# Gated linear attention on one Trainium2 core: unread products in TensorE's waits, and the head of the output stage beside the last chunk

## The reference

```python
def step(S, inp):                                  # one chunk of GLA
    b = jnp.cumsum(ax, axis=1)
    diff = b[:, :, None] - b[:, None, :]
    decay = jnp.where(causal, jnp.exp(jnp.minimum(diff, 0.0)), 0.0)
    scores = jnp.einsum('bthc,bshc,btshc->btsh', qx, kx, decay)
    o = jnp.einsum('btsh,bshe->bthe', scores, vx) + jnp.einsum('bthc,bhce->bthe', qx * jnp.exp(b), S)
    b_last = b[:, -1]
    S_new = jnp.exp(b_last)[..., None] * S + jnp.einsum('bshc,bshe->bhce', kx * jnp.exp(b_last[:, None] - b), vx)
...
of, Sf = gla_scan(gq, gk, gv, log_a[:, :, 0], S0[:, 0])
ob, Sb = gla_scan(flip(gq), flip(gk), flip(gv), flip(log_a[:, :, 1]), S0[:, 1])
og = rms_norm((of + flip(ob)), o_gain).reshape(B, T, GLA_WIDTH) * jax.nn.silu(gg)
out = jnp.concatenate([lru, og], axis=-1)
...
x = x + gate * rms_norm(out @ w_out, g)            # the output stage
```

## Time and profile before

| what | value |
| --- | --- |
| median of three runs | 3104.09 us (3102.58 to 3104.70) |
| the profiled execution's own time | 3103.27 us |
| its span, first to last instruction | 3101.5 us |
| mean granted clock of PE | 0.962 of 2.4 GHz |
| busy: PE, DVE, POOL, ACT | 2917.8, 2031.2, 1426.6, 1238.6 us |
| chain that ended last, by engine | PE 66%, POOL 12%, DVE 9% |
| GLA passes 0 to 8 | 2017.5 to 2210.6 us of the span |
| output stage of layer 1, first product | 2226.70 us |

### The profile page before, as it was taken

How to read it: one execution, slowest core, us unless ns; L and a number is a source line. 1 busy time by engine, 2 the same in 40 slices (tenths; PEclk the granted TensorE clock), 3 DMA queues, 4 the chain that set the end, 5 groups by cost and what they waited for, 6 DMA issues and landing times.

```text
span 3101.5 us, 41472 instructions
## 1 busy us (share of the span) xinstructions
PE 2917.8 (94%) x16141; PEld 2504.6 (81%) x16141; DVE 2031.2 (65%) x2488; ACT 1238.6 (40%) x2055; POOL 1426.6 (46%) x1002
## 2 busy tenths in 40 slices
PE   7999988999899999999999999989799999999998
PEld 3898876666689999978877887768689999978877
DVE  3679776554568444587877376578778544488886
ACT  2311164676543222233324477544353332333322
POOL 1121064666434444487851121176433443488870
PEclk9999998999999999999999999966799999999999
DMA  5566574000222323333243323241232323332241
GB/s 207 175 211 221 194 213 148 24 1 28 85 82 79 115 88 113 107 115 116 98 137 98 109 93 135 78 133 54 67 107 74 104 95 108 125 123 74 100 176 61
DMA packets 230880, 346.81 MB, mean 112 GB/s; under 512 B 32118, under 2 KB 124318, under 8 KB 230686
## 3 DMA queue, kind: packets, MB, share of 16 engines
q1 hardware_dynamic: 230686, 344.17, 33.2%
HBM read 259.18 MB, written 84.94 MB: 111 GB/s over the span
## 4 chain that ended last, share of the span: by engine, by line
PE 66%; POOL 12%; DVE 9%; issue 5%; ACT 4%; DMA 2%; SPq 1%; PEldq 0%; POOLq 0%; ACTq 0%; DVEq 0%; PEld 0%
PE psum L1002 19%; PE psum L1194 9%; POOL d_slot L1134 6%; PE psum L662 6%; PE psum L2950 5%; PE psum L1299 3%; PE psum L1647 3%; PE psum L665 3%; PE psum L1176 2%; PE psum L3964 2%; PE psum L439 2%; PE psum L2609 1%; DVE ada_acc L296 1%; PE psum L829 1%; PE psum L2590 1%
## 5 line engine op out<-in xcount | busy, mean ns | idle before, releaser
L1194 PE MATMUL psum<-d_slot 128*128 128x512 f32 x2016 | 468.1, 392 | 8.6 <-DVE yacc L1239 3.7
L1194 PEld LDWEIGHTS psum<-d_slot 128*128 128x128 f32 x2016 | 379.7, 189 | 92.9 <-DVE yacc L1239 5.3
L1002 PE MATMUL psum<-AT,w_slot 128*128 128x288 f32 x2688 | 369.1, 296 | 4.7 <-POOL w_slot L967 4.7
L1002 PEld LDWEIGHTS psum<-AT,w_slot 128*128 128x128 f32 x2688 | 362.6, 189 | 5.1 <-POOL w_slot L967 5.1
L1134 POOL TENSOR_TENSOR d_slot<-down_a,d_slot 128x512 fp32r<-128x512 f32 x168 | 300.1, 1810 | 72.2 <-ACT d_slot L1125 72.0
L591 POOL TENSOR_TENSOR WT<-RAW,WT 128x1024 fp32r<-128x1024 f32 (+3 forms) x30 | 111.1, 3726 | 429.5 <-ACT WT L580 429.5
L662 PE MATMUL psum<-WT,AT 128*128 128x512 f32 (+1 forms) x1296 | 282.5, 378 | 4.0 <-ACT stage L717 4.0
L1002 PE MATMUL psum<-s_hi,w_slot 128*128 128x288 f32 x1344 | 269.0, 295 | 3.3 <-issue 1.7
L662 PEld LDWEIGHTS psum<-WT,AT 128*128 128x128 f32 x1296 | 231.7, 190 | 46.8 <-ACT stage L717 4.3
L967 POOL TENSOR_TENSOR w_slot<-RAW,w_slot 128x512 fp32r<-128x512 f32 x112 | 155.8, 1402 | 224.1 <-ACT w_slot L963 224.1
L1002 PEld LDWEIGHTS psum<-s_hi,w_slot 128*128 128x128 f32 x1344 | 215.3, 188 | 4.1 <-issue 2.1
(11 more groups left out here) (467 smaller groups left out, 6083.6 us busy)
## 6 DMA issues: line engine op xcount, KB each, us to landing
RAW<-ffn_w SPq DMA_DIRECT2D x40, 1024.0 KB, 6.6
ada_raw<-ada_w SPq DMA_DIRECT2D x36, 1024.0 KB, 6.2
hidden<-hid SPq DMA_DIRECT2D x56, 576.0 KB, 3.1
down_a<-hidden SPq DMA_DIRECT2D x48, 512.0 KB, 5.9
RAW<-ffn_w SPq DMA_DIRECT2D x48, 512.0 KB, 7.4
RAW<-w_in_even SPq DMA_DIRECT2D x5, 2048.0 KB, 8.2
RAW<-w_in_odd SPq DMA_DIRECT2D x5, 2048.0 KB, 7.9
mix_x<-x_all SPq DMA_DIRECT2D x18, 512.0 KB, 3.3
```

The costliest lines, as they stand in the source:

```text
L1002: mm = nc.tensor.matmul(psum[:, bank + b, 0:HB], w_slot[p][:, w, k, :], TOKENS[p][x][:, k, b * HB:(b + 1) * HB], start=(begins and k == 0 ...
L1194: mm = nc.tensor.matmul(psum[:, D_RING[q % 3] + pair % 2, :], slot[:, 0, x, k, pair * P:(pair + 1) * P], slot[:, 1, w, k, :], start=(k == ...
```

## The change

Five things are altered, all in layer 1.

- PE issues products that nothing reads: `unread(n)` multiplies 128 x 128 of a weight group with its first 512 columns into bank 6. There are 8 behind `gl_go`, ahead of level 0 of pass 0, 6 behind that, and in every pass 4, 2, 1 and 1 behind levels 2, 3, 4 and 5. Bank 6 is also that of a state update, so PE waits for the backward state behind level 2.
- Tiles 0 and 1 are early in layer 1 too. ACT runs their sigmoid in passes 5 and 6 behind level 5's exponential. In pass 8, behind level 7's exponential and ahead of `keep_kT`, it sums their squares with its accumulator, takes the inverse root and scales `h_sum` in place (`weigh_scalar`). POOL forms the gate and multiplies it in behind its work of pass 8 (`gate_gpsimd`). PE turns both tiles between the backward state read and the state updates of pass 8, ACT and DVE split them.
- The barrier behind the passes, its drains and POOL's clearing of semaphores go, and so does a table load on ACT. Passes take their semaphores from other sets, and `S_in` is folded into `gt_in` (`gt_at`).
- The second weight group is split without the barrier: ACT copies its last half once all of `h_sum` is final, and its first half once the final state is stored; POOL takes the low part of the last half, DVE that of the first half.
- PE takes layer 0's order: first halves of products 0 and 1, then the second half of product 0. SP waits for the final `h_sum` ahead of the stage's loads, and for the stored state ahead of the MLP's weights.

```diff
         def is_early(l, t):
-            return l == 0 and t < 2
+            return t < 2
...
             if l:
-                mixed(0)
-                mixed(1)
-                product(0)
+                product(0, [0])
+                product(1, [0])
+                product(0, [1])
                 mixed(2)
...
-                if t == 0 and l == 0:
+                if t == 0:
                     product(1, [1])
...
+        def weigh_scalar(act, chain, t):
+            s, inv = t % 2, inverse_of(1, t)
+            act.wait_ge(gt_b_kept, SAMPLE_TILES - t)
+            for h in range(4):
+                ins = nc.scalar.activation(mo_junk[t][:, h, :], h_tile(t)[:, h, :], ACT.Square, accum_out=inv[:, h:h + 1])
+            ins.then_inc(mo_ssq[s], 1)
+            act.wait_ge(mo_ssq[s], 1)
+            chain.link(nc.scalar.activation(inv, inv, ACT.Ln, bias=eps[:, :], scale=1.0 / MD))
+            chain.link(nc.scalar.activation(inv, inv, ACT.Exp, scale=-0.5))
+            for h in range(4):
+                ins = nc.scalar.activation(h_tile(t)[:, h, :], h_tile(t)[:, h, :], ACT.Copy, scale=inv[:, h:h + 1])
+            ins.then_inc(mo_inv_ready[s], 1)
...
             if l:
-                nc.scalar.preload_act_table_set("natural_log_exp_and_others")
-                for t in range(2):
-                    sigmoid(t)
-                    inverse(t)
-                mixed(0)
-                split_high(act, 8 * l + 7)
-                mixed(1)
+                act.wait_ge(o_kept, TILES)
+                act.wait_ge(w_in, 16 * (8 * l + 8))
+                nc.scalar.activation(WT[:, 1, 0, LAST_HALF], RAW[:, LAST_HALF], ACT.Copy).then_inc(w_high, 1)
+                act.wait_ge(S_out, 32)
+                nc.scalar.activation(WT[:, 1, 0, FIRST_HALF], RAW[:, FIRST_HALF], ACT.Copy).then_inc(w_high, 1)
...
+        def gate_gpsimd(pool, t):
+            pool.wait_ge(mo_inv_ready[t], 1)
+            pool.wait_ge(mo_gated[t], 1)
+            nc.gpsimd.tensor_tensor(h_tile(t), h_tile(t), gate_of(1, t), ALU.mult).then_inc(mo_ready[t], 1)
...
+                    if step == 5 and v in (5, 6):
+                        sigmoid_scalar(act, chain, 1, v - 5)
                     if step == 7:
+                        if v == CTX:
+                            for t in range(2):
+                                weigh_scalar(act, chain, t)
                         keep_kT(v)
+            for t in range(2):
+                mixed_scalar(act, 1, t)
...
+            def unread(n):
+                for _ in range(n):
+                    nc.tensor.matmul(psum[:, T_BANK, :], WT[:, 0, 0, 0:P], WT[:, 0, 0, 0:512], start=True, stop=True)
...
+            UNREAD = {2: 4, 3: 2, 4: 1, 5: 1}
             pe.wait_ge(gl_go, 1)
             pe.drain()
+            pe.wait_ge(w_low, 15)
+            unread(8)
             begin(0)
+            unread(6)
             level(0, 1)
             for v in range(TILES):
                 for step in range(2, NL + 1):
                     level(v, step)
+                    if step == 2:
+                        pe.wait_ge(gt_S_new[1], v)
+                    if step < 6:
+                        unread(UNREAD[step])
                     if step == 6:
                         turn_keys(v)
                 pe.wait_ge(gt_b_kept, v)
                 from_state(v, 1, B_BANK, True).then_inc(gt_b, 1)
+                if v == CTX:
+                    for t in range(2):
+                        mixed_tensor(pe, 1, t)
                 for d in (1, 0):
                     into_state(v, d)
...
-                next_stage(sp, "GLA chunks")
```

More of the change, by code:

```diff
@@ L2916, in mixed_tensor @@
                 pe.wait_ge(exp_done, ALL_STEPS)
+            if l and t == 0:
+                for q in range(2):
+                    pe.wait_ge(wi_put[q], per_step(CTX, 6 + q) + 1)
+            if l and t == 2:
+                pe.wait_ge(o_kept, TILES)
             for b in range(4):
@@ L3190, in out_vector @@
             if l:
[L3191 to L3195, removed]
+                square(2)
+                square(3)
             else:
                 low(1)
[L3198 to L3202, removed]
+            half = FIRST_HALF if l else LAST_HALF
+            dve.wait_ge(w_high, 9 * l + 8)
+            nc.vector.tensor_tensor(WT[:, 1, 1, half], RAW[:, half], WTf[:, 1, 0, half], ALU.subtract).then_inc(w_low_rest, 1)
+            if l == 0:
                 dve.wait_ge(att_low, BATCHES)
-            square(2)
-            square(3)
+                square(2)
+                square(3)
             out(2)
@@ L3676, in trunk @@
         gt_in, gt_turned, gt_kT_kept, gt_b, gt_b_kept = (sem_of(n) for n in ("gt_in", "gt_turned", "gt_kT_kept", "gt_b", "gt_b_kept"))
-        S_in, S_out, S_reset = (sem_of(n) for n in ("S_in", "S_out", "S_reset"))
+        S_out, S_reset = (sem_of(n) for n in ("S_out", "S_reset"))
+        gt_at = lambda v: 32 + 48 * (v + 1)
         lru_high = sem_of("lru_high")
@@ L3722, in chunk_sync @@
             for par in range(2):
-                sp.dma_start(gl_S[64 * par:64 * par + 64, :, par * P:(par + 1) * P], A["gla_S"][par]).then_inc(S_in, 16)
+                sp.dma_start(gl_S[64 * par:64 * par + 64, :, par * P:(par + 1) * P], A["gla_S"][par]).then_inc(gt_in, 16)
             backward_load(sp, 0)
@@ L3747, in weigh @@
                 if d:
-                    pool.wait_ge(gt_in, v * 48 + 48)
+                    pool.wait_ge(gt_in, gt_at(v))
                     if v >= 2:
@@ L3783, in chunk_gpsimd, with chunk_scalar @@
                         copies(v + 1)
-        def chunk_scalar(act):
+            for t in range(2):
+                weigh_gpsimd(pool, 1, t)
+            for t in range(2):
+                gate_gpsimd(pool, t)
+        def chunk_scalar(act, chain):
             def state_exp(v, d, part):
@@ L3889, in new_state @@
                 if v == 0:
-                    dve.wait_ge(S_in, 32)
+                    dve.wait_ge(gt_in, gt_at(0))
                 if d:
@@ L3941, in chunk_vector @@
                     first_factors(v + 1)
+            for t in range(2):
+                low_vector(dve, 1, t)
             for step in (0, 5, 6):
@@ L3978, in from_state @@
                 if v == 0:
-                    pe.wait_ge(S_in, 32)
+                    pe.wait_ge(gt_in, gt_at(0))
                 if v == CTX:
@@ L3989, in into_state @@
                 if d:
-                    pe.wait_ge(gt_in, v * 48 + 48)
+                    pe.wait_ge(gt_in, gt_at(v))
                 values = gt_v if d else vals(v)
@@ L4052, in mixer_scalar @@
             else:
-                chunk_scalar(act)
-                next_stage(act, "GLA chunks")
+                chunk_scalar(act, chain)
         def mixer_tensor(pe, l):
```

32 lines of the change are left out of this document (18 added, 14 removed).

## The result

| | time, us | span, us |
| --- | --- | --- |
| before | 3104.11 (3102.58 to 3104.70) | 3101.5 |
| changed | 3075.24 (3074.72 to 3075.79) | 3072.7 |

The ratio is 0.9910, with a 95% interval of 0.9898 to 0.9922. The forecast was 3076.1, so its sum came out; two of its terms were off by 5 us each, in opposite directions.

The account below looks back on a forecast made before the run. The prediction took DVE, almost throughout, and PE, where its clock is slow, to bound a pass. Gains of 11 us in passes 1 to 7 and 17 up to tile 2 made 28, so 3104.1 became 3076.1 us; range 3069 to 3091.

Parts of the forecast that it names:

- Products, passes 1 to 7: Unread products in PE's gaps behind levels 2 to 5 keep the clock high, gaining 11.0 us over passes 1 to 7.
- added wait: PE's wait for the backward state behind level 2, in every pass: claimed to cost nothing.
- overrun: Four products behind level 2 exceed PE's gap by 0.4 us, costed at 0 with DVE as cover, 0.4 a pass without.
- the cap by DVE's busy time: Passes 1 to 7: gain limited to DVE's idle time, 16.3 us at most; 1.3 us each taken in passes 1 to 4.
- The 2.6 taken off: Passes 1 to 7: deduction of 2.6 us from a 13.6 us gain, as the clock should fall in some passes.
- Ahead of pass 0 and the sigmoids: 14 products before and in pass 0 cost 0, up to 2 us; gate activations in passes 5 and 6 cost 0, bound 1.
- Pass 8: Last pass with ACT's squares and POOL's gates: last product ends 0.7 us earlier net, bounds -2.5 and +3.
- The head: Start of layer 1's output stage: without barrier and late gates, tile 2 begins at 2238.3 and not 2255.34, 17 us gained.
- (a): Passes 1 to 7: transposes let the clock fall behind level 6, gaining 4 us in place of 11, 3083 us; chance 0.16.
- (b): Passes 1 to 7: clock not held at all, 6 us lost there, 8 us gained overall, 3096 us; chance 0.11.
- (c): All passes: 8 products each at half clock on the chain, 29 us lost against 14 gained, 3119 us; chance 0.03.
- (d): Output stage's start stalls more: POOL's split or ACT's late keys cost 5 us more, 3081 us; chance 0.07.

## Why the prediction was right, point by point

**Products, passes 1 to 7.** The direction and the mechanism were right: the clock is what they give. The added wait and the overrun cost nothing that shows: PE still waits 0.64 us behind the four products of level 2. The size was off: 11 us predicted, 16.2 measured, and 20.2 with more of them. The step that failed is the cap by DVE's busy time. I took 1.3 us a pass in passes 1 to 4 as DVE was busy for 74.33 of 81.10 us; these passes fell by 2.4 us each on average. In part that is PE's lead: between DVE's own merges they fell by 1.7 each. The rest of the error is that DVE's busy time is no floor: for the same 129 instructions it fell from 74.20 to 71.62, and that of the 56 factor products among them from 39.4 to 36.6. These take 0.42 alone and up to 1.50 beside POOL's products, so the busy time holds waits that change with the pass. A pass that kept its clock took 16.3 to 17.8 us and not 19. The 2.6 taken off for passes that lose the clock was too small: the two cost 4.0 in all (126.5 against 122.5).

One reading of the rows was short: of the gaps in pass 2, the 0.68 stands behind level 5, which took 1.27 and so already ran partly slow, and a gap of 0.59 before it was left out. No term used either.

**Ahead of pass 0 and the sigmoids.** Both at nothing, and so it was: pass 1 began at 2045.09 (2045.69 before). With ten products, passes 5 and 6, with the sigmoids in them, took 17.8 and 17.2 us beside 17.8 for passes 2 to 4.

**Pass 8.** Predicted 0.7 less, measured 4.6 more; outside even the bound of 2.5 that I gave. The step named the wrong engine. ACT's part was costed at 4.0 us a tile and took 3.1, and the keys waited for PE. What was missed is DVE, whose six factor products of levels 5 to 7 stood beside POOL's gate products, which I had put into POOL's idle time at no cost: 6.7 us and not 2.6. Measured from DVE's merge, pass 8 grew by 2.4, so some of these 4.1 us came back within the pass; its better clock (0.81 and not 0.69) fits that, but no run shows it alone. About half of the 4.6 is PE's lead, which counts as a gain in passes 1 to 7. The Trainium skill, "SBUF — State Buffer", section "SBUF: two separate sides", describes a lock on a shared pair of ports that a two-input DVE operation or a GpSimd operation holds for a whole instruction. The trace agrees, 0.42 alone and up to 1.50 beside POOL. I had weighed this for the weight split alone.

**The head.** Predicted 17 with pass 8's 0.7 in it, so 16.4 from the end of pass 8; measured 17.2, less 1.4 of slow clock in the product behind, of which the forecast had 0.8 in its 16.4: 15.8 against 16.4. The wait before the third half product was 0.32 (0.5 predicted), tile 3's 3.30 (3.3), the slow clock 1.4 (0.8). Layer 0's rows were the same order in the same code, and gave the new wait to 0.03 us. In the split POOL took 4.61 and DVE 4.41 us, where POOL had 6.67 and DVE 2.29. From POOL's start to the later end it is 6.8, the 6.67 of the forecast; only the order changed, so DVE's half and not POOL's is what PE waited for.

**Rivals.** (a) came in two of seven passes and is out as a rule: at ten products the clock holds through the transposes of seven passes. (b) did not come, and (c) came in parts: a pass that loses the clock early pays for its unread products, 24 to 25 us with 8 of them, 23.8 with 10, and 28.2 and 28.8 with 10 and 12 where POOL's moved products stand in it too. (d) did not. The sum was right because 5.2 us too little in the passes stood against 5.3 too little of cost in pass 8. Some 2 us of both is PE's lead, which only moves from one term to the other; that the rest cancels, a gain too small from DVE's busy time and the cost of POOL beside DVE left out, is luck. In which moment of an execution the clock is taken stays open; no run here measured that.

## What to carry to other kernels

Idle time of PE between small products can cost twice, once as a wait and once in the clock behind it. Unread products in these waits were paid back here, 16 us with 8 a pass, but their places matter: the same 8 spread evenly kept 5 us of that in the passes, and 1 us in the time, which is within the spread. Work moved into POOL's idle time is not free: look at what DVE does in that moment. And measure a stretch at the marks of the engine that bounds it, or the lead of another passes for a gain. Where the same order already runs elsewhere in the kernel, its rows there are the best price for it.

## What was not expected of the hardware

The same kernel loses the clock in different passes from one execution to the next: passes 3 and 5 in one, 2, 5 and 7 in the other, with executions from 3069.03 to 3077.22 us. A spread over four runs says little here, and a variant needs its trace. And a pass in which the clock is lost early with unread products in place (23.4 to 25.3 us) is 3 to 5 us longer than one that never had them (20.3), so a thing that helps by 2 to 3 us a pass on average can cost more than that in a single one. The pass behind it is short, 16 us, so that such a pair takes about 40 us, as two passes of before did. With POOL's moved products in the pass it was 28.8; how much of that is theirs is not measured.
